# Four column orders for the moving operand in a transformer MLP on one NeuronCore

## What is computed

```python
        x = x + rmsnorm(mixed, g[1])
        h = rmsnorm(x, g[2])
        m = jnp.square(jax.nn.relu(h @ w_up[l])) @ w_down[l]
        x = x + rmsnorm(m, g[3])
```

## Time and profile before

| | us |
|---|---|
| median of 2 runs | 2208.02 |
| lowest and highest run | 2207.98, 2208.05 |
| span of the profiled execution, first to last instruction | 2206.3 |
| TensorE busy in that span | 2197.4 |
| VectorE busy | 1509.1 |
| ScalarE busy | 1066.9 |

### The profile page before, as it was taken

One profiled execution on the slowest core, in us unless ns is written; L12 is line 12 of the kernel. 1 busy time (PEld: TensorE's weight loads), 2 busy tenths in 40 slices (PEclk: granted clock), 3 DMA queues, 4 the chain that ended last, 5 costly groups with the idle time before them and its releaser, 6 DMA issues.

```text
span 2206.3 us, 37987 instructions
## 1 busy us (share of the span) xinstructions
PE 2197.4 (100%) x16122; PEld 2068.7 (94%) x16122; DVE 1509.1 (68%) x1910; ACT 1066.9 (48%) x1418; POOL 63.1 (3%) x72
## 2 busy tenths in 40 slices
PE   9999999999999999999999999999999999999998
PEld 9999999999999889989988988998889999999987
DVE  7789588888889657544554555555766656577776
ACT  5444445544444546444443543444656555444443
POOL 1000000000000000000000000000100000010001
PEclk9999999999999999999999999999999999999999
DMA  8876676788787755656656666656664445678784
GB/s 275 241 225 209 192 247 221 228 281 258 256 278 264 241 182 182 195 194 194 192 195 195 183 202 203 197 186 207 235 196 148 135 144 172 216 264 294 251 281 156
DMA packets 248034, 475.00 MB, mean 215 GB/s; under 512 B 21526, under 2 KB 26000, under 8 KB 247096
## 3 DMA queue, kind: packets, MB, share of 16 engines
q1 hardware_dynamic: 243032, 454.40, 64.7%
q0 software_dynamic: 4832, 18.16, 2.5%
HBM read 468.30 MB, written 5.78 MB: 215 GB/s over the span
## 4 chain that ended last, share of the span: by engine, by line
PE 99%; issue 0%; DVE 0%; ACT 0%; POOLq 0%; POOL 0%; DVEq 0%
PE ps L888 21%; PE ps L889 21%; PE ps L890 21%; PE ps L881 11%; PE ps L882 11%; PE ps L883 11%; PE ps L805 1%; PE ps L705 1%; PE ps L794 0%; PE ps L674 0%; PE ps L902 0%; PE ps L717 0%; PE ps L784 0%; PE ps L785 0%; PE ps L783 0%
## 5 line engine op out<-in xcount | busy, mean ns | idle before, releaser
L888 PE MATMUL ps<-op0h,whiW 128*128 128x256 f32 x3376 | 936.8, 277 | 0.0
L890 PE MATMUL ps<-op0h,wloW 128*128 128x256 f32 x3376 | 932.3, 276 | 0.0
L889 PE MATMUL ps<-op0l,whiW 128*128 128x256 f32 x3376 | 932.2, 276 | 0.0
L1279 DVE TENSOR_TENSOR wloW<-raw,whiW 128x1024 fp32r<-128x1024 f32 (+1 forms) x503 | 611.0, 1227 | 339.0 <-ACT whiW L935 336.9
L935 ACT ACTIVATE whiW<-raw 128x1024 fp32r<-128x1024 f32 (+1 forms) x504 | 529.0, 1058 | 581.1 <-PE ps L890 482.8
L888 PEld LDWEIGHTS ps<-op0h,whiW 128*128 128x128 f32 x3376 | 633.7, 188 | 2.2 <-issue 1.6
L889 PEld LDWEIGHTS ps<-op0l,whiW 128*128 128x128 f32 x3376 | 633.8, 188 | 0.5
L890 PEld LDWEIGHTS ps<-op0h,wloW 128*128 128x128 f32 x3376 | 633.7, 188 | 0.0
L1279 DVE TENSOR_TENSOR wloT<-raw,whiT 128x1024 fp32r<-128x1024 f32 (+1 forms) x264 | 317.4, 1211 | 249.5 <-ACT whiT L935 248.0
L935 ACT ACTIVATE whiT<-raw 128x1024 fp32r<-128x1024 f32 (+1 forms) x264 | 273.7, 1046 | 291.0 <-PE ps L883 243.0
L881 PE MATMUL ps<-whiT,op1h 128*128 128x512 f32 x640 | 249.2, 389 | 0.0
(11 more groups left out here) (308 smaller groups left out, 2070.2 us busy)
## 6 DMA issues: line engine op xcount, KB each, us to landing
raw<-in_w_in SPq DMA_DIRECT2D x256, 512.0 KB, 4.4
raw<-in_w_up SPq DMA_DIRECT2D x128, 512.0 KB, 3.7
raw<-in_w_down SPq DMA_DIRECT2D x128, 512.0 KB, 4.0
raw<-in_w_ada SPq DMA_DIRECT2D x96, 512.0 KB, 4.7
raw<-in_w_gate SPq DMA_DIRECT2D x96, 512.0 KB, 4.8
raw<-in_w_out SPq DMA_DIRECT2D x64, 512.0 KB, 5.1
raw<-in_w_branch SPq DMA_DIRECT2D x48, 512.0 KB, 4.9
raw<-in_w_proj_a SPq DMA_DIRECT2D x24, 512.0 KB, 5.7
```

Source lines behind the costliest of these rows:

```text
L888: pe.matmul(o, wh, xh[:, ka, :], start=first and m % 2 == 0, stop=False, skip_group_check=True)
L889: pe.matmul(o, wh, xl[:, ka, :], start=False, stop=False, skip_group_check=True)
L890: mm = pe.matmul(o, wl, xh[:, ka, :], start=False, stop=last, skip_group_check=True)
L1279: v.tensor_tensor(wlo[job.mode][q % NSPL][:, :, 0:job.n], x, h.bitcast(F32), ALU.subtract).then_inc(s_lo, 1)
```

## The change

`chunk` takes a column order `way` from the block number: 0 for every job outside the MLP and for MLP block 0, and 1, 2, 3 for blocks 1, 2, 3. In `ordered`, way 1 goes over the columns from last to first (step -1). Way 2 splits the columns into two halves and takes 2 columns of the first half, 2 of the second, the next 2 of the first, and so on; way 3 does the same by 8 columns. The same order is given to the output in PSUM, so every result lands where it did. The stationary operand, the number of matmuls, the semaphores and the other engines are as before.

```diff
+            def ordered(x, way):
+
+                if way == 1:
+                    return x[:, ::-1]
+                if way > 1:
+                    return x.rearrange("p (h a r) -> p a h r", h=2, r=(2, 8)[way - 2])
+                return x
+
             def chunk(q, tts=(0, 1), half=None):
                 job, k = chunks[q]
+                way = job.arg[0] if job.ep in ("up", "dn") else 0
...
-                            pe.matmul(o, th, h[:, kk, c0:c1], start=first, stop=False, skip_group_check=True)
-                            pe.matmul(o, th, l[:, kk, c0:c1], start=False, stop=False, skip_group_check=True)
-                            mm = pe.matmul(o, tl, h[:, kk, c0:c1], start=False, stop=last, skip_group_check=True)
+                            o, mh, ml = (ordered(x, way) for x in (o, h[:, kk, c0:c1], l[:, kk, c0:c1]))
+                            pe.matmul(o, th, mh, start=first, stop=False, skip_group_check=True)
+                            pe.matmul(o, th, ml, start=False, stop=False, skip_group_check=True)
+                            mm = pe.matmul(o, tl, mh, start=False, stop=last, skip_group_check=True)
...
-                            pe.matmul(o, wh, xh[:, ka, :], start=first and m % 2 == 0, stop=False, skip_group_check=True)
-                            pe.matmul(o, wh, xl[:, ka, :], start=False, stop=False, skip_group_check=True)
-                            mm = pe.matmul(o, wl, xh[:, ka, :], start=False, stop=last, skip_group_check=True)
+                            o, mh, ml = (ordered(x, way) for x in (o, xh[:, ka, :], xl[:, ka, :]))
+                            pe.matmul(o, wh, mh, start=first and m % 2 == 0, stop=False, skip_group_check=True)
+                            pe.matmul(o, wh, ml, start=False, stop=False, skip_group_check=True)
+                            mm = pe.matmul(o, wl, mh, start=False, stop=last, skip_group_check=True)
```

## The result

The changed kernel takes 2311.24 us (2 runs, 2310.48 to 2312.01) against 2208.02: ratio 1.0467, 95% interval 1.045 to 1.0484. It is 103 us slower.

A forecast was written before the change was run, and what follows sets the result against it. TensorE's matmul spacing was taken to bound the kernel: a 2206.3 us span plus 7.7 for the reversed block and 0 for the two blocks of halves, plus 1.7 outside the span, gave 2216 us, range 2185 to 2385.

The forecast's parts named there:

- the likeliest case: All three reordered MLP blocks stay near the plain cost, 2177 to 2246 us, most likely 2216; chance 0.52.
- The bound: Whole kernel: the time is the sum of TensorE's instruction costs; other engines matter only if they stop feeding it.
- Last to first: Block 1, reversed columns: one step of 6.7 ns more on each of 1152 matmuls, 7.7 us.
- By 8: Block 3, halves in turn by 8 columns: 0 taken, in the middle of -10.3 and +12.8 us.
- By 2: Block 2, halves in turn by 2 columns: 0 taken, in the middle of -10.3 and +12.8 us.
- only the order by 2 falls behind: Rival, block 2: each jump costs a column's time or more, 81.9 us, kernel 2290 to 2372; chance 0.09.
- Half pace for the reversed block: Rival, block 1: neighbouring columns are paired only when they rise, so 164 us more, kernel 2372; chance 0.14.
- any order slows matmuls: Rival from the skill page on non-contiguous PSUM: two or three blocks at half pace, 2536 to 2699 us; chance 0.15.
- Repeated meetings with the weights: Rival, blocks 1 to 3: moving columns and weights meet repeatedly, 26.7 ns per matmul, kernel 2240 to 2300; chance 0.09.
- The steps of 6.7 ns: Sign in the MLP blocks' matmul spacings: they differ from before by multiples of 6.7 ns, the time of 16 columns.

## Why the prediction was right and where it wasn't

The measured 2311 us lies inside 2185 to 2385, at ratio 1.047. But the likeliest case said 2216, no change that can be told, and that case didn't happen. The range reached so far up to hold one slow block, with 0.14 for the reversed one and 0.09 for the one by 2. One block was slow, by 2, but not by the mechanism given for it, and two others added 20 us. That the time lies inside owes more to the width of the range than to its reasoning, and is in good part luck.

- *The bound.* Right. TensorE's spacing sets the time, block 0 and everything outside the MLP kept theirs, and no wait moved onto the path.
- *Last to first.* Forecast 7.7 us, 120 and 233.4 ns; measured 6.5 us, 118.5 and 233.3. The size was right, and the reason isn't borne out: with a quarter of the weights it is still 117.8 and 233.3, and groups of 8 columns that rise inside pay the same when the groups fall.
- *By 8.* Forecast 0 with an upper bound of 12.8; measured 13.8, at 16 and 30 ns leftover. Just past the bound, because `dn` has more than the 20 ns of `ub`.
- *By 2.* This is the step that failed: "For the two blocks of halves I take 0". It was 82.4 us, 80% of the difference. It rested on the earlier trace rows, and neither bears on it. `ub` reads its stationary operand with step 2 and pays 6.7 ns; the moving operand with step 2 pays 225 ns for 512 columns. L827 has runs of 128, and runs of 64 and more are free. The rival "only the order by 2 falls behind", with 81.9 us for the block and 2290 us for the kernel, had the right block and nearly the right price; with the other two blocks it would have given 2310. It got 0.09. The price was right by luck, since its mechanism, one column's time for every jump, fell at runs of 4 (126.6 ns, not 136 to 143) and at runs of 1 (112.9, where every column jumps).
- *Half pace for the reversed block*, and *any order slows matmuls*, didn't come. Of the latter, the PSUM half is refuted for the orders tried. The read half is too broad: by 64 and swapped pairs are plain, and by 1 is faster.
- *Repeated meetings with the weights* didn't come: no `up` stood at 130 to 150 ns, and fewer weights made nothing faster.
- *The steps of 6.7 ns* were a sign to look for, and most spacings don't keep to them: `up` rose by 5.1 and 9.6 ns in blocks 1 and 3, and places on the grid gave 4.4 and 5.3. Places did matter, but none made mode T faster.

**What is shown:** the cost is all on the read of the moving operand; for runs of 2 it doesn't depend by more than 3 ns on the distance between the places from 32 bytes on, and it doesn't go away with a quarter of the weights; runs of 4 that begin on a 16-byte line escape most of it, and runs of 4 that don't, pay as runs of 2.

**What stays open:** why single columns from two places are read at full pace, 4 places at 140 ns and pairs from two places at 1.5 times, what the 6 to 17 ns of runs from 8 to 32 are, and why the same order by 2 takes 166.7 or 170.0 ns. Three theories (a time per run, 64-byte pieces, two kept lines) each failed at one point at least. Single columns on the PSUM side weren't tried.

## What to carry to other kernels

If columns of a matmul must be permuted, do it in the PSUM pattern: in the orders tried (by 2, and last to first) it cost nothing, while the order by 2 on the moving read made the matmul nearly half as long again. On the moving side keep runs of at least 4 float32 that begin on 16 bytes, better 64 columns. Avoid gaps, which cost about twice; whether a copy that closes them pays was not tried. And price an access pattern only from a row with the same operand in the same role.

## What was not expected of the hardware

- Moving columns with gaps, of one column or of fourteen, cost about twice: 228.8 and 451.2 ns at step 2, 217.8 and 486.7 for pairs 64 bytes apart, against 113.4 and 226.7.
- Single columns from two places in turn are read faster than plain: 215.8 ns for 512 columns, 2.5 over the 213.3 of 2.4 GHz, against 226.7. The same pair of columns over and over reads 111.7 ns for 256.
- Loading 32 instead of 128 stationary columns shortened the load from 188 to 109 ns in `dn` and left the matmul's spacing at 231.6, no less than 226.7.
